# Decay exponents kept in three buffers, their column added by ScalarE in pieces of 128, identities written in the last positions of a slot

## What is computed

```python
decay = jnp.exp(jnp.where(incl, gc[..., :, None] - gc[..., None, :], -jnp.inf))
kb = k * beta[..., None]
a_mat = jnp.where(strict, jnp.einsum("bhncd,bhnmd->bhncm", kb, k) * decay, 0.0)
t_mat = a_mat + jnp.eye(cs, dtype=f32)
sol = lax.linalg.triangular_solve(t_mat, rhs, left_side=True, lower=True, unit_diagonal=True)
qk = jnp.einsum("bhncd,bhnmd->bhncm", q, k) * decay
...
s = s * d_i[..., None, None] + jnp.einsum("bhcd,bhce->bhde", k_i, v_new)
```

## Time and profile before

| | us |
|---|---|
| median of 3 runs | 3356.7 |
| lowest and highest | 3348.37, 3357.59 |
| the profiled execution's own time | 3356.15 |
| its span | 3354.4 |
| PE busy | 3133.7 (93%) |
| DVE, ACT, POOL busy | 1884.8 (56%), 1461.9 (44%), 825.8 (25%) |

### The profile page before, as it was taken

The page is one execution under the profiler, slowest core; times in us unless marked ns, Lnnn a source line. Parts: engine busy times, 40 slices in busy tenths (PEclk is TensorE's granted clock), DMA queues, the critical chain, the costliest instruction groups (busy, mean ns, idle before and its releaser), DMA issues. The chain is left out here.

```text
span 3354.4 us, 56002 instructions
## 1 busy us (share of the span) xinstructions
PE 3133.7 (93%) x22057; PEld 2045.9 (61%) x22057; DVE 1884.8 (56%) x3609; ACT 1461.9 (44%) x2963; POOL 825.8 (25%) x588
## 2 busy tenths in 40 slices
PE   5879999999999999999999999897999999999998
PEld 2347776777767764455545565444777676667663
DVE  1147676767676762234542344345777777777742
ACT  3125445544544451145532444333555554555521
POOL 0023433433343320001101011002433434343400
PEclk9789999999999999999999999898999999999999
DMA  9811211221121116112302111202111222121135
GB/s 376 307 56 48 60 54 43 63 56 55 44 68 50 48 46 218 67 46 62 128 16 57 32 45 40 80 2 70 57 58 58 62 59 62 52 73 52 52 109 193
DMA packets 224098, 261.96 MB, mean 78 GB/s; under 512 B 19418, under 2 KB 158948, under 8 KB 223716
## 3 DMA queue, kind: packets, MB, share of 16 engines
q1 hardware_dynamic: 223844, 258.46, 23.9%
HBM read 239.15 MB, written 19.27 MB: 77 GB/s over the span
## 5 line engine op out<-in xcount | busy, mean ns | idle before, releaser
L895 PE MATMUL ps<-hT,W 128*128 128x512 f32 (+1 forms) x2656 | 999.1, 506 | 5.5 <-ACT arena L1128 3.5
L895 PEld LDWEIGHTS ps<-hT,W 128*128 128x128 f32 x2656 | 471.3, 193 | 203.7 <-issue 172.1
L1314 DVE CAST_PREDICATED arena<-mask,ps 128x384 bf16<-128x384 uint32 x448 | 252.3, 563 | 184.3 <-PE ps L964 176.6
L1145 ACT CAST arena<-ps 128x384 bf16<-128x384 f32 x384 | 167.8, 482 | 364.8 <-PE ps L951 363.6
L2349 PE MATMUL ps<-arena 128*128 128x512 f32 x712 | 311.1, 595 | 2.8 <-SPq L192 2.8
L1316 DVE CAST_PREDICATED arena<-mask,ps 128x384 bf16<-128x384 uint32 x448 | 250.2, 558 | 0.0
L2349 PEld LDWEIGHTS ps<-arena 128*128 128x128 f32 x712 | 134.6, 191 | 167.6 <-issue 162.6
L1984 PE MATMUL ps<-hT,W 128*128 128x512 f32 (+1 forms) x608 | 218.2, 493 | 0.8 <-DMA W<-in_att_w_in 0.6
L1433 POOL TENSOR_TENSOR arena<-arena,cst 128x768 f32<-128x768 f32 x64 | 117.0, 1850 | 390.2 <-DVE arena L1283 390.2
L1474 POOL TENSOR_TENSOR arena<-arena 128x768 f32<-128x768 f32 (+1 forms) x32 | 49.2, 1537 | 613.4 <-DVE arena L1377 613.4
L1295 DVE SCALAR_TENSOR_TENSOR arena<-arena,vec 128x770 f32<-128x770 f32 (+1 forms) x192 | 195.4, 1017 | 6.8
(11 more groups left out here) (280 smaller groups left out, 6288.8 us busy)
## 6 DMA issues: line engine op xcount, KB each, us to landing
arena<-in_ada_w SPq DMA_DIRECT2D x24, 2048.0 KB, 19.5
W<-in_gdn_w_in SPq DMA_DIRECT2D x95, 512.0 KB, 4.0
arena<-decay_sums SPq DMA_DIRECT2D x64, 384.0 KB, 3.9
W<-decay_rows SPq DMA_DIRECT2D x64, 384.0 KB, 5.0
arena<-in_gdn_w_out SPq DMA_DIRECT2D x32, 512.0 KB, 10.5
W<-in_gdn_w_out SPq DMA_DIRECT2D x30, 512.0 KB, 3.4
arena<-gated SPq DMA_DIRECT2D x32, 384.0 KB, 7.7
gated<-arena SPq DMA_DIRECT2D x24, 384.0 KB, 2.4
```

What stands on the lines that cost most here:

```text
L895: mm = pe.matmul(ps[:, b, 0:t1 - t0], w[:, i, :], env.hT[:, i, t0:t1], start=(i == 0), stop=(i == KD - 1))
L1145: act.copy(half_cols(Xb[d], s, d), ps[:, 2 * d, 0:384].rearrange("p (c b s) -> p c b s", c=NT, s=s)).then_inc(*inxe.up(m, lv, d))
L1314: dve.copy_predicated(half_cols(Mb[d], s, d), wide(env.m4[:, d, lv]), src_m).then_inc(*inm.up(m, lv, d, "m"))
```

## The change

1. `gexp` has three buffers (`m % 3`). SP loads, and POOL caps, the exponents of unit n+3 in slot n; so unit 1 is loaded and capped in slot -2.
2. `exponents` and its semaphore are gone from DVE. ACT adds the column as the bias of the exponential: a bias is one value per partition and instruction, and the column differs by chunk, so each direction becomes six instructions of 128 columns. They stand at position 3 (direction 0) and position 5 (direction 1) of slot n for unit n+2; for unit 0 at position 13 of slot -2.
3. `matrix` moves to position 12 in odd slots. In even slots it stays at the end, since it needs the `KK` of position 17.
4. ACT writes the results of `t1` and `t2` into `NATb` and `NLOb` instead of `Mb` and `MTb`. So POOL can write the identities for the next unit after `r0` and after `m1` (DVE L1325) of the same slot, and they stand in its order behind the decayed q and ahead of the copy of k. Those for unit 0 are written right after `capped(0)`.

The diff, cut to its core:

```diff
-G_AT = 11
-EXP_AT = 13
+EXP_AT = (3, 5)
+NAT_AT = 12
...
             def load_g(m):
...
-            if n > -2 and n + 2 in U:
-                sp.wait_ge(gcap.sem, gcap.at(n + 1, 1))
+            if n + 3 in U:
+                sp.wait_ge(gcap.sem, gcap.at(n + 2, 1))
                 sp.wait_ge(qkd.sem, qkd.at(n, 1))
-                load_g(n + 2)
+                load_g(n + 3)
...
-                        mm = pe.matmul(unit(d, c), Xb[d][:, c], Mb[d][:, c], start=False, stop=True, skip_group_check=True)
+                        mm = pe.matmul(unit(d, c), Xb[d][:, c], NATb[d][:, c], start=False, stop=True, skip_group_check=True)
...
-                        mm = pe.matmul(unit(d, c), Xb[d][:, c], MTb[d][:, c], start=True, stop=True)
+                        mm = pe.matmul(unit(d, c), Xb[d][:, c], v.NLOb[d][:, c], start=True, stop=True)
...
-        def decay(m):
-
-            for d in BOTH:
-                act.wait_ge(garg.sem, garg.at(m, d))
-                act.activation(v.gexp[m % 2][:, d], v.gexp[m % 2][:, d], ACT.Exp).then_inc(*gexp.up(m, d))
+        def decay(m, d):
+
+            act.wait_ge(gcap.sem, gcap.at(m, d))
+            for c in range(NT):
+                g = v.gexp[m % 3][:, d, cols(c)]
+                ins = act.activation(g, g, ACT.Exp, bias=sc_col(COL, c, m, d))
+            ins.then_inc(*gexp.up(m, d))
...
-                if p == G_AT and n + 2 in U:
-                    exponents(n + 2)
+                if p == NAT_AT and n % 2 and n + 2 in U:
+                    matrix(n + 2)
...
-            if n + 2 in U:
+            if n % 2 == 0 and n + 2 in U:
                 matrix(n + 2)
...
+        def ones_on_diagonal(m):
+
+            for d in BOTH:
+                pool.wait_ge(rf.sem, rf.at(m - 1, "r0", d))
+                pool.tensor_copy(Mb[d], idb).then_inc(*minit.up(m, d, "m"))
+            for d in BOTH:
+                pool.wait_ge(m1.sem, m1.at(m - 1, d))
+                pool.tensor_copy(MTb[d], idb).then_inc(*minit.up(m, d, "t"))
+
+        capped(0)
+        ones_on_diagonal(0)
...
                     pool.tensor_tensor(NAT[d], NAT[d], NATb[d], ALU.subtract).then_inc(*nlo.up(m, d, "rest"))
                     pool.wait_ge(nlo.sem, nlo.at(m, d, "rest"))
+                    pool.wait_ge(rf.sem, rf.at(m - 1, "t3", d))
                     pool.tensor_copy(v.NLOb[d], NAT[d]).then_inc(*nlo.up(m, d, "mid"))
...
-            if n + 2 in U:
-                capped(n + 2)
+            if n + 3 in U:
+                capped(n + 3)
...
+            if m in U and m + 1 in U:
+                ones_on_diagonal(m + 1)
```

34 lines of the change are left out of this document (13 added, 21 removed).

## The result

| | before | after |
|---|---|---|
| median of the runs of this comparison, us | 3356.07 (4 runs) | 3295.06 (4 runs) |
| lowest and highest | 3348.37, 3357.59 | 3291.22, 3295.89 |
| profiled execution, span | 3354.4 | 3293.5 |
| PE busy | 3133.7 (93%) | 3108.8 (94%) |
| DVE, ACT, POOL busy | 1884.8, 1461.9, 825.8 | 1745.3, 1522.9, 775.7 |

The changed kernel takes 0.982 of the time, with a 95% interval from 0.9803 to 0.9837: 61 us less. The forecast was 3322, 34 us less, within 3303 to 3343.

What follows compares the result with a forecast made beforehand. PE's own instructions were taken to set the pace, leaving only its idle time to win: 3356.15 - 53.6 (closed waits and tails) + 3.5 (late values) + 9.7 (starts) + 7 (what is late next) = 3322.8; predicted 3322 us, range 3303 to 3343.

Steps and rivals of the forecast that it cites:

- PE sets the pace, and the gain is PE's idle time: Steady slots: only PE's idle time can be won, 36 us in layer 0, 23 in layer 3, plus the layers' starts.
- sum of closings: Waits of PE expected to close: 14 and 12.6 us in layer 0, 13 and 4 in layer 3.
- Who closes the seams: Seams between slots: moving odd matrices and early identities close 14 of 15.1 us in layer 0, 13 of 17.1 in layer 3.
- L1128: Layer 0, norm's bank emptied by ACT: moving the exponentials from position 13 shortens PE's waits there, 12.6 us less.
- Tails: Split rows of matmuls: each closed wait gives 0.18 us beyond its idle time, 16 in layer 0, 40 in layer 3: 10 us.
- Layer 0's clock: Granted clock of 0.99 in layer 0: no term in the sum; one rival said less time if it goes to full.
- Twelve small exponentials: ACT, positions 3 and 5: six take 1.7 us; values late by about 0.5 us in 7 odd slots of layer 3, 3.5 us more.
- Start of the layers: Slot -2: the square begins 4.9 us later in layer 3, 2.8 in layer 0; with the exponentials' cost, 9.7 us more.
- What is late next: Seams: once DVE ends no wait, PE may meet low parts, a bank or slowed scores; 7 us taken off the gain.
- What would show it: Signs: idle by L1351 under 2 us, by L1316 under 5; two slots in 128 to 129 (layer 0), 111 to 112 (layer 3).
- all closes and nothing follows: Rival for the whole kernel: no 7 us, values never late, a start that costs 5: 3307 us or less; chance 0.1.
- The first rival: Seams: the waits only move, 27 of the 53.6 us are won, 3.5 and 9.7 lost: near 3341 us; chance 0.2.

Runs made afterwards that it cites:

- e9_casts: Kernel before with the identities written early, plus four POOL casts per seam into a tile nobody reads: 3359.64 us, ratio 1.0014.
- e10_memsets: Kernel before with the identities written early, plus four POOL memsets per seam into a tile nobody reads: 3309.94 us, ratio 0.9863.
- e6_exp13: Changed kernel with every matrix at the end of its slot and all twelve exponentials at position 13: 3377.76 us, ratio 1.0073.
- e7_pieces64: Changed kernel with each exponential cut into two of 64 columns, 24 per unit in place of 12: 3305.37 us, ratio 0.9845.

## Why the prediction was right or wrong, point by point

- **PE sets the pace, and the gain is PE's idle time**: right. The idle time in the inner pieces fell by 26.8 and 18.0 us, against 26.6 and 17 in the sum of closings. In layer 0 that is partly luck: the waits that the sum named gave 12.3 and 11.3, 23.6 us, and the other 3 came from small waits that it did not name (L1009, L939).
- **Who closes the seams**: wrong in its reasons, right in its size. The step of the mechanism that failed is "At an even seam the matrix stays, but alone it takes 2 x 0.95 us ... worth 0.6 to 1.2 us at the seam", and with it "at the odd seams the 2.52 us of L1344 go" as the reason for the odd ones. I took POOL's company to slow the matrix only, and let the scores "keep part of their 3.35 us". The even seam gives 1.9 us, the identities alone close 22.3 of layer 3's 23.9, and e9_casts against e10_memsets shows why. At the odd seams, too, the low parts did not "start at once and run beside the scores": they start 0.7 us behind them, and the scores take 1.29 us. The forecast's own sentence, that two such streams slow each other down and that moving POOL is worth as much, was the right one, and I did not carry it into the sum.
- **L1128**: right. Exponentials alone take the waits from 13.9 to 5.0, 0.85 each where 0.7 was forecast; e6_exp13 shows that the place does it.
- **Tails**: 10 us were forecast. Busy time fell by 16.6 in layer 0, of which 8.5 are clock; the other 8 and the 5.9 in layer 3, 14 in all, I put down to tails. The times that PE idled, short ones too, fell in the two inner pieces from 65 to 38 and from 86 to 58, 27 and 28 fewer where 16 and 40 were forecast: layer 0 was undercounted and layer 3 overcounted. At 0.18 us each that is 9.9; of the 4 us beyond it no row shows the cause.
- **Layer 0's clock**: the step that failed by most: the sum put it at nothing, and only a half-sentence in a rival named it. It gave 8.5 us, the largest single miss.
- **Twelve small exponentials**: the price was 1.7 us for six and is 1.86, the estimate by the Trainium skill's page "ScalarE: Activation LUTs", section "What ACT_TABLE_LOAD costs". Its consequence, "the values are late by about 0.5 us: 7 slots, 3.5 us more", was wrong: it set the six against the 0.91 us before L1102 alone. In the odd slots ACT had idled 1.64 us in all on the way to the values (0.46 + 0.91 + 0.27), and they are as early as before (4.70 against 4.83 us into the slot). What the Trainium skill's page "VectorE: DVE Perf Modes" says in its section on the TRN2 errata, that small pieces pay a fixed latency each, agrees with e7_pieces64 (0.25 us for 64 columns, 0.31 for 128); at positions 3 and 5 PE did not wait for it.
- **Start of the layers**: 9.7 us forecast, 13.4 measured (6.3 + 7.1). The mechanism is right: the square began 6.0 us later in layer 3 against 4.9, since the load landed about 5 us behind its issue, over a microsecond more than the median of 3.9 in the profile's page. In layer 0 the wait grew by 3.6 against 2.8, and the rest there is a longer stretch at half clock behind it.
- **What is late next**: the second step that failed. "I take off 7 us" for a follower had no row behind it and was a guess. The only wait that is new in the steady slots is L973's in layer 3, 1.8 us, and none came in layer 0.
- **Layers 1 and 2**: 0 forecast, 6.5 found. It is the clock again (26.9 us at the lower level before, 10.1 after), and kernels without any part of the change vary as much (806.2 to 811.7), so this part of the result is luck as far as the runs show. Without it the changed kernel is some 54 us faster, near 3302, still just below the range.
- **What would show it**: L1316 under 5 (2.6) and two slots of layer 3 in 111 to 112 us (111.7) were met; L1351 under 2 was not (2.8), and two slots of layer 0 took 126.6, below the forecast 128 to 129, by the clock and the tails.

The misses add up: clock 8.5, layers 1 and 2 6.5, follower 7, late values 3.5, tails 4, idle time 1, against 3.7 more at the starts, 27 us in all. All but the last lie on one side. So the steps of the sum that failed are the clock, which it put at nothing and which gave 8.5 us in layer 0, and the two costs with no row that bore them out, the follower (7 us; 1.8 of new waits, already within the idle time's fall) and the late values (3.5; none). The range reached to 3303 since it was built around costs and had no entry for the clock. The rival "all closes and nothing follows", 3307 "and less if layer 0's granted clock goes to full", had a chance of 0.1 and is the one that came, though not in its "start that costs 5", which was 13.4. The first rival's sum was off by 1: 3356.15 - 27 + 3.5 + 9.7 is 3342, not 3341.
